# Order and spacing of ScalarE's side work in a fused two-block transformer kernel

## The reference

```python
h = rmsnorm(x, norm_mix_g); proj = h @ w_in            # a_q a_k a_v b_q b_f b_i b_g c_q c_kv c_kr gate_logits
y_a = softmax(a_q a_k^T / 8 + bias(relative position)) @ a_v      # "attention A", 8 heads of 64, causal by chunks of 64
y_b = hgrn2(silu(b_q), b_f, b_i) ... * silu(b_g)                  # gated linear recurrence
y_c = latent attention from c_q, c_kv, c_kr                       # 8 heads, keys of 96
gates = sigmoid(gate_logits)                                      # 3 branches x 1024
x = x + (sum over branches of gates * (y @ w_branch)) @ w_out
x = x + relu(rmsnorm(x) @ w_ff1)^2 @ w_ff2
```

## Time and profile before

| what | value |
|---|---|
| median of 3 runs | 2276.05 us (2275.41 to 2276.76) |
| profiled execution | 2277.32 us |
| its span, first to last instruction | 2275.6 us |
| mean granted TensorE clock | 0.996 |
| TensorE matmul busy | 2220.9 us, 98% |
| VectorE, ScalarE, GpSimd busy | 1200.1, 940.3, 219.6 us |

### The profile page before, as it was taken

How to read it: one execution, slowest core, us unless ns; L and a number is a source line. 1 busy time by engine, 2 the same in 40 slices (tenths; PEclk the granted TensorE clock), 3 DMA queues, 4 the chain that set the end, 5 groups by cost and what they waited for, 6 DMA issues and landing times.

```text
span 2275.6 us, 26925 instructions
## 1 busy us (share of the span) xinstructions
PE 2220.9 (98%) x10484; PEld 1733.9 (76%) x10484; DVE 1200.1 (53%) x1827; ACT 940.3 (41%) x1561; POOL 219.6 (10%) x312
## 2 busy tenths in 40 slices
PE   8989999999999999999999999999999999999999
PEld 6658788667888888877565788888887657888887
DVE  4573664555544444473445555545545685555454
ACT  4463433455443223243545533333435565333331
POOL 0000121211210000030323200000120001000000
PEclk9999999999999999999999999999999999999999
DMA  5212111212323222322011232222321112332233
GB/s 171 74 42 88 47 37 63 68 38 102 102 93 100 96 96 98 102 84 93 29 56 38 74 102 93 95 100 93 102 93 65 56 47 68 101 101 92 93 102 102
DMA packets 52111, 187.48 MB, mean 82 GB/s; under 512 B 5905, under 2 KB 6033, under 8 KB 51857
## 3 DMA queue, kind: packets, MB, share of 16 engines
q1 hardware_dynamic: 51984, 185.76, 24.6%
HBM read 183.64 MB, written 2.10 MB: 82 GB/s over the span
## 4 chain that ended last, share of the span: by engine, by line
PE 89%; DVE 4%; ACT 4%; issue 2%; POOL 1%; DMA 1%; SPq 0%; ACTq 0%; DVEq 0%; POOLq 0%
PE ps L925 22%; PE ps L928 21%; PE ps L926 21%; PE ps L946 4%; PE ps L949 3%; PE ps L947 3%; PE ps L1269 2%; PE ps L910 2%; PE ps L1120 1%; PE ps L1153 1%; PE ps L1257 1%; PE ps L1245 1%; ACT wh L1321 1%; PE ps L1273 1%; PE ps L1033 1%
## 5 line engine op out<-in xcount | busy, mean ns | idle before, releaser
L1321 ACT CAST wh<-raw 128x1024 fp32r<-128x1024 f32 (+1 forms) x336 | 353.0, 1051 | 874.1 <-PE ps L928 758.3
L925 PE MATMUL ps<-hh,wl 128*128 128x512 f32 x1408 | 566.9, 403 | 14.6 <-DVE wl L1642 13.2
L928 PE MATMUL ps<-hl,wh 128*128 128x512 f32 x1408 | 551.2, 391 | 0.0
L926 PE MATMUL ps<-hh,wh 128*128 128x512 f32 x1408 | 550.4, 391 | 0.0
L1642 DVE TENSOR_TENSOR wl<-raw,wh 128x1024 fp32r<-128x1024 f32 (+1 forms) x336 | 416.4, 1239 | 191.5 <-ACT wh L1321 190.4
L925 PE MATMUL ps<-R,wl 128*128 128x512 f32 x896 | 359.5, 401 | 7.3 <-issue 5.8
L928 PE MATMUL ps<-R,wh 128*128 128x512 f32 x896 | 350.6, 391 | 0.0
L926 PE MATMUL ps<-R,wh 128*128 128x512 f32 x896 | 350.1, 391 | 0.0
L925 PEld LDWEIGHTS ps<-hh,wl 128*128 128x128 f32 x1408 | 265.7, 189 | 73.3 <-issue 20.4
L928 PEld LDWEIGHTS ps<-hl,wh 128*128 128x128 f32 x1408 | 265.4, 188 | 56.9 <-DVE hl L1721 0.3
L926 PEld LDWEIGHTS ps<-hh,wh 128*128 128x128 f32 x1408 | 265.8, 189 | 55.9 <-issue 2.9
(11 more groups left out here) (225 smaller groups left out, 2195.5 us busy)
## 6 DMA issues: line engine op xcount, KB each, us to landing
raw<-in_weights SPq DMA_DIRECT2D x332, 512.0 KB, 3.3
x<-in_x_t SPq DMA_DIRECT2D x4, 512.0 KB, 7.2
F<-in_x_t SPq DMA_DIRECT2D x4, 512.0 KB, 4.6
out<-x SPq DMA_DIRECT2D x8, 256.0 KB, 2.1
raw<-in_weights SPq DMA_DIRECT2D x4, 416.0 KB, 3.1
x<-in_bias SPq DMA_DIRECT2D x1, 1024.0 KB, 6.2
C<-in_consts SPq DMA_DIRECT2D x1, 832.0 KB, 6.8
F<-in_weights SPq DMA_DIRECT2D x2, 384.0 KB, 3.6
```

The costliest lines, as they stand in the source:

```text
L925: pe.matmul(out, lo[:, k, cs], xh, start=k == 0, stop=False)
L926: pe.matmul(out, hi[:, k, cs], xh, start=False, stop=False)
L928: last = pe.matmul(out, hi[:, k, cs], xl, start=False, stop=k == u.nk - 1)
L1321: act.copy(B.wh[s][:, 0:nk * ncol], B.raw[s][:, 0:nk * ncol]).then_inc(S["w_hi"], 1)
```

## The change

Four parts. (1) In attention A, ScalarE's copy of the turned weights stands ahead of the exponential of the same side tick; the latent attention keeps its order. (2) For `bq`, `bg` and `gate` units the three activations of the logistic stand one per tick: the first Exp in the evaluation, Ln one tick later, the last Exp two ticks later; `fgate` keeps its three in a row. (3) `ev2`, VectorE's product, moves from one tick to three ticks after the evaluation. (4) `uB` and `uF` are one list of 64 dense ticks; the 39 side ticks of attention A run beside the first 36 of it, 39/36 for each, so four ticks of `uF[0]` are in it, and the other 28 run alone.

```diff
@@ ready
-        if u.ev in ("bq", "bg"):
-            self.defer(1, "ev2", u)
+        if u.ev in ("bq", "bg", "gate"):
+            self.defer(1, "sig2", u)
+            self.defer(2, "sig3", u)
+        if u.ev in ("bq", "bg"):
+            self.defer(3, "ev2", u)
@@ make
-        self.run(interleave(self.dense(uB), self.attn(ATTN["A"]), 39 / 32))
         uF[0].banks, uF[1].banks = [0, 1, 4, 5], [2, 3, 6, 7]
-        self.run(self.dense(uF))
+        made = list(self.dense(uB + uF))
+        self.run(interleave(iter(made[:36]), self.attn(ATTN["A"]), 39 / 36))
+        self.run(made[36:])
@@ scalar_program, sigmoid
         act.activation(w[:], bank[:], ACT.Exp, scale=-1.0).then_inc(S["ev_a"], 1)
+        if u.ev == "fgate":
+            sig2(u)
+            sig3(u)
+
+    def sig_tile(u):
+        return B.W[u.arg["at"] % 4 if u.ev == "gate" else u.arg["wk"]]
+
+    def sig2(u):
         at.wait_ge("ev_a", u.act[0])
-        act.activation(w[:], w[:], ACT.Ln, bias=one).then_inc(S["sig"], 1)
+        act.activation(sig_tile(u)[:], sig_tile(u)[:], ACT.Ln, bias=one).then_inc(S["sig"], 1)
+
+    def sig3(u):
         at.wait_ge("sig", u.sig - 1)
-        act.activation(w[:], w[:], ACT.Exp, scale=-1.0).then_inc(S["sig"], 1)
+        act.activation(sig_tile(u)[:], sig_tile(u)[:], ACT.Exp, scale=-1.0).then_inc(S["sig"], 1)
@@ scalar_program, attn
     def attn(a, n):
+        if a.name == "A" and 0 <= n - a.t < a.nt:
+            turned(a, n - a.t)
         i = n - a.e
         if 0 <= i < a.nt:
...
-        if 0 <= n - a.t < a.nt:
+        if a.name != "A" and 0 <= n - a.t < a.nt:
             turned(a, n - a.t)
```

More of the change, by code:

```diff
@@ L1624, in scalar_program @@
     todo = {"begin": begin, "late": late, "split": split, "first": first, "root": root, "root2": root2, "merge": merge, "at": attn, "df": diff, "df_soft": diff_soft, "df_norm": diff_norm,
-            "ev": ev, "ev_low": ev_low, "bf": bf,
+            "ev": ev, "ev_low": ev_low, "sig2": sig2, "sig3": sig3, "bf": bf,
             "h_decay": h_decay, "h_exp": h_exp, "h_sq": h_sq, "h_ms": h_ms, "h_low": h_low, "c_norm": c_norm, "c_q": c_q,
```

## The result

The changed kernel takes 2252.84 us (median of 4 runs, 2252.35 to 2253.49) beside 2275.73 for the kernel before (2271.81 to 2276.76): a ratio of 0.9903, 95% interval 0.9886 to 0.9920. The medians are 22.9 us apart and the ratio makes it 22, outside the range on record (2257 to 2270.5) on the fast side. The case "everything goes" (2256) lies nearest and still falls short. The profiled executions have spans of 2275.6 and 2251.2 us: 24.4 us to explain.

What follows compares the result with a forecast made beforehand. TensorE was taken to bound the kernel, busy 2220.9 of 2275.6 us. Gains of 9.8 us in the first attention's stage and 2.5 in the latent attention, 12.3 together, gave 2263.7 us against the median of 2276.05; range 2257 to 2270.5.

Steps and rivals of the forecast that it cites:

- everything goes: Rival: no residue, both clock falls gone, 4 us in the latent attention; 2256 us, chance 0.13.
- The stage can give 16.3 us at most.: First attention: eleven waits for the copy cost 13.1 us with lost tails, two clock falls 3.2 us.
- 2.0 us stay: Attention A: copy waits remaining because VectorE lags in heavy items, 0.5 us for each of four groups.
- 2.1 us, new: First attention: the later product frees a projection's bank late, new waits of 0.7 us at three of eight units.
- 0.8 us: First attention: one doubled side tick without scores or product between its two transposes shows its copy, costing 0.8 us.
- one gone, 1.6 us: First attention: with waits of 1 us left, one of two clock falls disappears, giving 1.6 us.
- Beside the recurrence ... TensorE has no wait to give.: Gates' logistic beside the recurrence and in the pure gate stage: no TensorE wait to remove, gain 0.
- Latent attention "2.5": Latent attention: spreading the logistic shortens four waits, 3.3 us less 0.8 for copies meeting a single piece; bounds 0.3 and 5.
- the price is nothing: ScalarE: Ln standing alone between copies and softmax exponentials causes no extra activation table loads, cost 0.
- nothing arrives: Rival: new bank waits, a whole tick for most units, give back the copies' gain; 2276 us within 4, chance 0.08.
- slower: Rival: the copy holds the exponential and VectorE's reciprocal waits, 13 us against 6.6 gained; 2282.5 us, chance 0.04.
- the copy's waits: Sign: in the first attention, transposes' waits for ScalarE's copy fall from 11.3 to 2 to 4 us.

Runs made afterwards that it cites:

- e9: Changed kernel with VectorE taking each of attention A's 32 reciprocals twice, the extra result unused; 2253.21 us, ratio 0.9909.
- e8: Changed kernel with the product that frees a projection's bank four ticks after the evaluation instead of three; 2257.81 us, ratio 0.9924.
- e2: Kernel before with only the logistic spread over three ticks and its product moved two ticks later; 2260.49 us, ratio 0.9931.
- e6: Changed kernel with the logistic back in one tick and its product's move taken back; 2266.03 us, ratio 0.9965.
- e12: Changed kernel, unedited, measured and profiled once more; 2253.23 us, ratio 0.9904.

## Why the prediction was wrong

The mechanism and the direction were right; the sizes were not. By the prediction's own steps:

- *"The stage can give 16.3 us at most."* Right within 0.6 us: waits, 0.16 for each and the falls account for all eight combinations, with 134 us left. Two readings under it are off. The falls were dated 1.1 us too early: the clock was down from 122.9 and from 146.8, 1.2 and 0.7 us after the waits had ended, and TensorE was busy through both; the 0.66 came from windows that began too soon, not from rounding. And a sixth wait, 0.35 us at 119.02, also stands behind a logistic: 6.2 us behind logistics and 5.1 behind late maxima.

```profile
122.90:126.30 3.40, 3.40 (x11) 0.50 0.00 0
146.80:150.20 3.40, 3.40 (x11) 0.50 0.35 128
```

- *"2.0 us stay"* (four heavy groups at 0.5). **Wrong, the first failed step.** No wait of this kind is left. From the changed kernel's trace, the scaled weights of the eight 512-key items are ready 1.0 to 2.9 us before their transposes start. The estimate let VectorE fall 2.3 us behind and left a residue although its own slack was 3.1, without a reason; e9 shows that even 4.6 us more work costs 0.2.
- *"2.1 us, new"* for the projection's bank. **Wrong.** No such wait. The products of four units end 0.9 to 1.2 us before the next use of the bank. Both this and the step above rest on VectorE's lag of 2.3 us against a slack; at the bank, slack less lag is 1.6 us more than the prediction had (0.9 ahead, not 0.7 behind). Which of the two was mis-sized the runs don't separate. e8 shows the wait one tick later, at 3.8 us for four units.
- *"0.8 us"* for a doubled tick with nothing between its transposes. The size is right, 0.74 and 0.16, but by luck: no doubled tick of the trace has nothing between its transposes, and the wait that stayed stands behind a cast and the logistic's first Exp.
- *The clock, "one gone, 1.6 us".* Both went, some 3 us. In seven of the eight combinations of the table the clock has at most one fall in this stretch; only the kernel before has two.
- Together: waits 12.2 instead of 8.2, clock 3.0 instead of 1.6, so 15.2 us instead of 9.8.
- *"Beside the recurrence ... TensorE has no wait to give."* **Wrong, an overlooked wait.** No row of the prediction shows the recurrence; the one wait there, 1.29 us, ended at 255.94. e2 and e6 show that the spread logistic removes it.
- *Latent attention "2.5", bounds 0.3 and 5.* **Too small, and outside the bounds**: 5.7. Of 6.5 us of waits, 1.6 are left. The 3.2 us between are these: 0.8 taken off for copies that meet a single piece, which cost nothing; 0.8 for five vanished waits at 0.16 each, not counted; 0.7 of the wait of 1.39 at 515.86, halved, which went whole; and 0.9 of two waits left out, 0.68 at 450.34 and 0.19 at 438.10. None of these three waits names the logistic; by the timeline its delay reached the two longer ones through VectorE's queue, and e2 shows that all three go with it.

```profile
450.34 0.70 PE L1009 MATMUL ps<-F 96*128 96x256 f32 x2 [0.68 <-ACT W L1445]
...
515.86 1.08 PE L1033 MATMUL ps<-F 128*64 128x512 f32 x4 [1.39 <-ACT F L1462]
```

- *The fall of the clock at 235.6* had no term. It is absent in the changed profile, 1.3 us; but e12 has one at that place, so it is not the change's doing for certain.
- *Order of functions: "the price is nothing".* Right: the changed kernel has as many table loads as before, and no stretch pays for Ln standing alone.

The rivals: "nothing arrives" and "slower" did not happen; in the first stretch no reciprocal waits for an exponential at all: VectorE's waits there are for TensorE, for high parts that ScalarE casts and, once, 1.9 us, for the logistic of a recurrence's gate. Of the signs named, the copy's waits were to be 2 to 4 us (0.7), L946's first start 13 us earlier (19.3: 177.14 and 157.82), VectorE over 80% busy (87%), at most one fall of the clock (none), L1565 no longer waited for by over 0.5 us (0.25).

The time of the kernel before varies from 2271.3 to 2278.8 us over all these runs, that of the changed kernel from 2251.6 to 2253.6. The runs of before near 2271.5 (eight of 41) have a mean granted clock of 0.998, those near 2276 of 0.995 or 0.996; the changed kernel has 0.998, once 0.999. So up to 4 of the 22 us go with falls of the clock that most executions of the kernel before have and those of the changed kernel do not; the rest is work that no longer waits.

## What to carry to other kernels

In an in-order queue, work that is ready and that the bounding engine waits for belongs ahead of work that still has to wait, and a block of dependent activations belongs spread over as many ticks as its consumer allows (one tick further, e8, and the bank is late): here, by the medians, the second gave 15.6 us alone and the first 6.8, and taken out of the whole they cost 13.2 and 1.3. Measure one part alone and one undone before crediting it, and list the clock's falls of each profile before adding up: here they made parts that nearly add look as if they overlapped by 7 us, and made a repair of 2.5 us look like 5.5. And when a residue is estimated from an engine's lag, read from the trace how long a result lies ready before it is used instead of adding up durations: the sums used here were 1.6 us off at the bank and carried two of the terms that failed.

## What the hardware showed that I had not expected

The clock's falls depend on the waits and also on something that differs between executions of one kernel. With the same 1.55 us wait (at 352.9 and at 355.2) the clock fell in one execution and not in the other, and eight of 41 runs of the kernel before take 4 us less than the rest, at a mean clock of 0.998 and not 0.995 to 0.997. In the first profiles of the two kernels, the last 10 us apart, each of the nine falls lasted 3.4 us at 1.2 GHz and began 0.2 to 1.2 us after a wait of TensorE (1.5 to 2.9 us) had ended; not every such wait was followed by one (1.67 us at 491.87 was not). A difference of 1.5 us between two single profiles may be one such fall; the first stretch less its falls repeats to 0.1 us. What decides between them is open.
